# Six FFNs of a two-block model: the exchange of half of x through memory issued by ScalarE instead of SyncE

## The reference, cut to what matters

```python
def swiglu(h, w_gate, w_up, w_down):
    return (jax.nn.silu(h @ w_gate) * (h @ w_up)) @ w_down

def hybrid_layer(x, ...):
    x = x + 0.5 * swiglu(rmsnorm(x, ffn1_norm), ffn1_wg, ffn1_wu, ffn1_wd)
    ...                                   # attention and gated linear attention, x = x + ... @ w_out
    x = x + 0.5 * swiglu(rmsnorm(x, ffn2_norm), ffn2_wg, ffn2_wu, ffn2_wd)
    return x
```

## Time and profile before

| | us |
|---|---|
| median of 3 runs | 1962.08 |
| lowest and highest of them | 1962.0 and 1962.49 |
| the profiled execution | 1962.03 |
| its span in the trace | 1960.2 |

### The profile page before, as it was taken

How to read it: one execution, slowest core, us unless ns; L and a number is a source line. 1 busy time by engine, 2 the same in 40 slices (tenths; PEclk the granted TensorE clock), 3 DMA queues, 4 the chain that set the end, 5 groups by cost and what they waited for, 6 DMA issues and landing times.

```text
span 1960.2 us, 27186 instructions
## 1 busy us (share of the span) xinstructions
PE 1947.4 (99%) x11074; PEld 1638.0 (84%) x11074; DVE 1381.7 (70%) x1714; ACT 1051.5 (54%) x1326; POOL 44.4 (2%) x73
## 2 busy tenths in 40 slices
PE   9999999999999999999999999999999999999998
PEld 8888988888888888888888898788888889878887
DVE  7666987666666697766666679776667666977665
ACT  6545575445544657544644467654454446765444
POOL 0120004000000000000000000000000000000000
PEclk9999999999999999999999999999999999999999
DMA  8765547666666544666566644466666664546662
GB/s 323 259 227 191 171 154 242 226 225 204 241 226 223 187 156 175 233 226 225 180 234 225 220 170 156 151 213 224 228 216 229 225 226 158 174 141 214 225 226 78
DMA packets 162494, 403.06 MB, mean 206 GB/s; under 512 B 94801, under 2 KB 116561, under 8 KB 119873
## 3 DMA queue, kind: packets, MB, share of 16 engines
q1 hardware_dynamic: 160448, 397.19, 58.6%
q0 software_dynamic: 1488, 3.78, 0.6%
q10 hardware_dynamic: 432, 0.35, 0.1%
HBM read 376.12 MB, written 22.81 MB: 204 GB/s over the span
## 4 chain that ended last, share of the span: by engine, by line
PE 92%; DVE 4%; DMA 1%; ACT 1%; SPq 1%; DVEq 1%; issue 0%; ACTq 0%
PE bank L513 87%; DVE w_lo L1479 1%; PE bank L558 1%; DMA raw<-stream 1%; SPq L422 0%; DMA arena<-spill_x 0%; DVE h_lo L1505 0%; PE bank L875 0%; PE bank L755 0%; PE bank L771 0%; DVE arena L1641 0%; PE bank L674 0%; PE bank L894 0%; PE bank L744 0%; PE bank L856 0%
## 5 line engine op out<-in xcount | busy, mean ns | idle before, releaser
L1479 DVE TENSOR_TENSOR w_lo<-raw,w_hi 128x2048 fp32r<-128x2048 f32 x330 | 755.8, 2292 | 356.5 <-ACT w_hi L1036 356.0
L1036 ACT ACTIVATE w_hi<-raw 128x2048 fp32r<-128x2048 f32 x330 | 629.6, 1909 | 267.5 <-PE bank L513 264.3
L513 PE MATMUL bank<-w_hi,h_hi 128*128 128x512 f32 x1552 | 607.7, 392 | 4.0 <-DVE h_lo L1505 2.8
L513 PE MATMUL bank<-w_hi,h_lo 128*128 128x512 f32 x1552 | 604.3, 389 | 0.0
L513 PE MATMUL bank<-w_lo,h_hi 128*128 128x512 f32 x1552 | 604.0, 389 | 0.0
L513 PEld LDWEIGHTS bank<-w_hi,h_hi 128*128 128x128 f32 x1552 | 291.3, 188 | 69.2 <-issue 6.8
L513 PEld LDWEIGHTS bank<-w_hi,h_lo 128*128 128x128 f32 x1552 | 291.3, 188 | 61.3
L513 PEld LDWEIGHTS bank<-w_lo,h_hi 128*128 128x128 f32 x1552 | 291.4, 188 | 59.5
L513 PE MATMUL bank<-w_hi,act_hi 128*128 128x512 f32 x832 | 326.8, 393 | 0.1
L513 PE MATMUL bank<-w_hi,act_lo 128*128 128x512 f32 x832 | 324.1, 390 | 0.0
L513 PE MATMUL bank<-w_lo,act_hi 128*128 128x512 f32 x832 | 323.8, 389 | 0.0
(11 more groups left out here) (245 smaller groups left out, 1359.6 us busy)
## 6 DMA issues: line engine op xcount, KB each, us to landing
raw<-stream SPq DMA_DIRECT2D x331, 1024.0 KB, 4.9
spill<-scratch SPq DMA_DIRECT2D x71, 256.0 KB, 3.6
scratch<-spill SPq DMA_DIRECT2D x71, 256.0 KB, 2.7
spill_x<-x SPq DMA_DIRECT2D x12, 256.0 KB, 2.6
arena<-spill_x SPq DMA_DIRECT2D x12, 256.0 KB, 2.8
arena<-arena SPq DMA_DIRECT2D x32, 64.0 KB, 2.9
arena<-rpb POOLq DMA_DIRECT2D x16, 66.5 KB, 4.4
x<-xt SPq DMA_DIRECT2D x1, 1024.0 KB, 15.2
```

The lines of the kernel that those rows point to most:

```text
L513: last = mm(o, a, r, start=start and n == 0, stop=stop and n == len(pairs) - 1)
L1036: fn(w_hi[u % SLOTS][:, :], raw[u % RAW][:, :], ACT.Copy).then_inc(hi_done, 1)
L1479: tt(w_lo[u % SLOTS][:, :], raw[u % RAW][:, :], w_hi[u % SLOTS][:, :].bitcast(F32), ALU.subtract).then_inc(lo_done, 1)
```

## The change

The four DMAs of each of the six exchanges leave SyncE's loop and go to ScalarE's program. ScalarE issues the two writes between its squares of piece 2 and piece 3, and the two reads between its split of back 0 and its split of front 0 + 3. Waits, sizes, shapes and semaphores are the same. SyncE's loop goes from one load to the next in these places.

```diff
@@ -395,17 +395,6 @@
-            def swap_x(b, L, j):
-
-                no = SWAPPED.index((b, L, j))
-                for t in range(2):
-                    wait_x(sp, x_no(b, L, 2 * j), 2 + t)
-                    sp.dma_start(spill_x[t].rearrange("c p h -> p c h"), x[:, t, 512:D].rearrange("p (c h) -> p c h", c=8)).then_inc(x_out, 16)
-                sp.wait_ge(x_out, 32 * (no + 1))
-                for t in range(2):
-                    sp.dma_start(x_landed[:, t, :].rearrange("p (q n) -> p q n", q=2),
-                                 spill_x[t].rearrange("(q c) (r a) h -> (c r) q (a h)", q=2, a=4)).then_inc(x_back, 16)
@@ -423,13 +412,10 @@
-            swapped = {ffn_use(b, L, j, "front", 0) + RAW: (b, L, j) for b, L, j in SWAPPED}
...
-                if u in swapped:
-                    swap_x(*swapped[u])
@@ -1062,6 +1048,19 @@
+            def swap_out(b, L, j):
+
+                for t in range(2):
+                    wait_x(act, x_no(b, L, 2 * j), 2 + t)
+                    act.dma_start(spill_x[t].rearrange("c p h -> p c h"), x[:, t, 512:D].rearrange("p (c h) -> p c h", c=8)).then_inc(x_out, 16)
+
+            def swap_back(b, L, j):
+
+                act.wait_ge(x_out, 32 * (SWAPPED.index((b, L, j)) + 1))
+                for t in range(2):
+                    act.dma_start(x_landed[:, t, :].rearrange("p (q n) -> p q n", q=2),
+                                  spill_x[t].rearrange("(q c) (r a) h -> (c r) q (a h)", q=2, a=4)).then_inc(x_back, 16)
@@ -1111,8 +1110,11 @@
                     turned_hi(b, L, 2 * j, [0, 1])
-                    squares(v, [2, 3])
+                    squares(v, [2])
+                    swap_out(b, L, j)
+                    squares(v, [3])
                     split(use_of("back", 0))
+                    swap_back(b, L, j)
                     split(use_of("front", 0) + SLOTS)
                     turned_hi(b, L, 2 * j, [2, 3])
```

## The result

| | us |
|---|---|
| before, median of 4 runs (lowest, highest) | 1962.28 (1962.0, 1963.1) |
| after, median of 4 runs (lowest, highest) | 1993.12 (1990.42, 1994.2) |
| ratio, 95% interval | 1.0154 (1.0141 to 1.0166) |
| profiled execution after, and its span | 1992.31, 1990.4 |
| profiled execution before, and its span | 1962.03, 1960.2 |

The kernel became slower by 30.8 us, 1.5%. Forecast were 7.6 us, and a range that ended at 1975. The direction was right, the size was not. The spans differ by 30.2 us, and these are to be found.

A forecast was written before the change was run, and what follows sets the result against it. TensorE's matmuls bound the kernel. Losses of 1.0 us in exchanges 1 and 4, 1.7 in 2, 1.4 in 3, 2.0 each in 5 and 6 make 9.1, less 1.5 lost today: +7.6, 1969.7 us; range 1961.5 to 1975.

The forecast's parts named there:

- What bounds the kernel, and the yardstick: TensorE bounds the kernel; each exchange is judged by its stage, line 558 to line 674, 22.57 us where nothing waits.
- T: Per exchange, start of line 558 (544 after) to VectorE's first block turn of x's right half; no TensorE wait up to 10.7.
- All that can be won is 1.5: All six exchanges: TensorE's waits for x cost about 1.5 us of 1962 today, so no more can be gained.
- each us beyond costs one us of the kernel: In each exchange, every us of T above 10.7 lengthens the kernel by one us.
- Writes, ScalarE, SyncE: Exchanges: writes cost 0 (bounds 0 to 0.4 us), ScalarE's wait 0; SyncE's next load comes earlier, which wins nothing.
- Sharing: Reads beside SyncE's load on two queues: 2.0 us added in exchanges 1, 4, 5, 6; 1.7 in 2 and 3.
- The sentence by the Trainium skill's rule: Engines alternate between queues packet by packet, so the reads would bear the load's whole time, 2.5 to 3 us.
- The fetch: An instruction fetch during the reads of exchanges 5 and 6 comes again and adds 1.0 us to each.
- No change: Rival: the reads, issued first, keep their place ahead of the load; 1960.5 to 1964, best 1962; chance 0.27.
- Faster: Rival: the fetch leaves the reads' way or the reads stand behind nothing, so 1.5 us return: 1960.5; chance 0.05.
- ScalarE issues late: Rival: ScalarE's DMA starts only after its split ends, so reads start 0.6 us later, behind the load: 1973.3; chance 0.13.

The follow-up runs named there:

- f1: Changed kernel, but only the writes go to ScalarE; SyncE issues the two reads and then the next load, as before the change: 1962.86 us, ratio 1.0001.
- g2: Changed kernel, but SyncE's next load also waits until the two writes have landed, so load and reads are issued together: 1987.38 us, ratio 1.0129.
- f3: Changed kernel, but SyncE's next load also waits until the reads have landed: 1962.47 us, ratio 0.9999.
- f4: Changed kernel, but ScalarE issues the load beside the reads, right behind them on the same queue: 1963.08 us, ratio 1.0002.
- g3: Kernel before the change, all on SyncE's one queue, but with the next load issued ahead of the two reads: 1985.26 us, ratio 1.0119.
- g4: Changed kernel plus 40 small matmuls at the start of TensorE's program, which moves later instruction fetches: 1984.05 us, ratio 1.0111.
- h1: Changed kernel, but the second load, the one after next, waits until the reads have landed: 1977.78 us, ratio 1.0081.
- h3: Changed kernel plus 19 small filler matmuls on TensorE before its wait in each of exchanges 2, 3, 5 and 6: 1985.71 us, ratio 1.0116.
- h2: Changed kernel, but the load beside the reads is issued as two DMAs of 512 KB: 1983.94 us, ratio 1.0113.

## Why the prediction was wrong in size

**What bounds the kernel, and the yardstick.** Right. Line 544 to line 660 is longer in all six places, and the six together carry the whole difference. T beyond 10.7 is paid in full: in exchange 1, 12.5 - 10.7 = 1.8, and the stage is 24.4 - 22.6 = 1.8 longer. "All that can be won is 1.5" holds too: no version here is faster than before by a measurable amount. The words "each us beyond costs one us of the kernel" failed where the wait was long: there it cost a slower clock on top.

**Writes, ScalarE, SyncE.** Right. The writes cost 0 (f1). The reads were issued at 308.08 in exchange 1, and the load at 308.44, for which 308.45 was said. In exchange 2 the load came at 492.24, which is the forecast 490.4 plus the 1.8 us that exchange 1 had already lost, 0.69 us ahead of the reads (0.85 was said).

**Sharing: the mis-sized term.** Taken were 2.0 us (1.7 in exchanges 2 and 3). Measured is 12.5 - 9.7 = 2.8 us in exchanges 1 and 4, where nothing else comes in: near the upper bound of 3 that the prediction gave and then dismissed, because it "leaves no worth to any head start". The reasoning for 2.0 was that a read in front keeps a part of its place. The rows show that the first read keeps all of it and the second none, and only the second one counts. The prediction had the fact in hand, that the load becomes free before the second read is issued, and drew nothing from it. By this alone the sum would be 6 x 1.8 = 10.8 less 1.5, so +9.3 us. The sentence by the Trainium skill's rule, 2.5 to 3 us, was nearer than the value taken. Its 32 packets of a read are those of both reads (one read is 256 packets, 16 for an engine), and the packet-by-packet turns that it describes show in g2, but not from 310.5 to 312 of after, where the load is alone.

**The fetch: the step that failed.** It was counted with 1.0 us, in exchanges 5 and 6 alone. In 2 and 3 the prediction did not see it, though it was there, 4.6 and 4.7 us into the stage of before and among the writes; only the T of 10.7 and 10.4 that it started from held its small cost there. Measured, together with the second load: 3.1 in exchanges 2 and 3, 3.6 and 3.2 in exchanges 5 and 6; 13.1 in all. The prediction priced the fetch and a load each by itself, on the traffic of before, and had no term for what two late things do to one engine. It never looked at the second load, 2.6 us behind the first.

**The clock: the missing step.** 7.8 us. No row of before has a wait of TensorE long enough to show it. Nothing in the prediction asked what TensorE does after it has stood still; the cost of it was put at nothing without a reason.

So 10.8 + 13.1 + 7.8 - 1.5 = 30.2 us, against 9.1 - 1.5 = 7.6. Which part is shown: the first by f3, f4 and g3; the second by g4 and h1; the third by h3, in one place. Open is why one engine comes to be late with its reads and then has the second load's packets among them: this is only seen in the packets, and no run tests it. Open is also by what rule the sixteen engines serve two queues: turns of whole DMAs are refuted (h2), the order of issue fits nearly everywhere, and g2 shows packets one for one.

**The rivals.** *No change* is refuted: the first read did keep its place, as it said, and this saved nothing. *Faster* has nothing for it. *ScalarE issues late* is refuted by the timeline of ScalarE: the reads are issued at 308.08 while the split of 306.77, which takes 1.92, still runs:

```profile
306.77 1.92 ACT L1022 ACTIVATE w_hi<-raw 128x2048 fp32r<-128x2048 f32 x1 [0.16 <-issue]
```

The range took its upper end from the one late mechanism that it knew, and had no room for costs that multiply.

## What to carry to other kernels

When a small transfer with somebody waiting for it is taken out of a queue, ask first what large transfer it had been holding back; here that was worth 31 us, and one wait on the load (f3) or one queue for both (f4) gives all of it back. Once TensorE is made to wait for several microseconds, price the matmuls after the wait as well. And a delay of one engine's share is not added to the others but can be multiplied by whatever else is queued by then, so the count of loads issued within the transfer's time belongs into the sum.

## What the runs showed of the hardware

- DMAs on two queues mostly passed in the order in which they were issued: 0.64 MB of a load in 1.5 us with no packet of the other queue between (100.7% of 16 engines), and the second read, issued 0.03 us behind that load, after it. Two half-loads issued ahead of the reads both went first (h2, exchange 2). Where load and first read were issued 0.09 us apart, their packets could alternate one for one, 60 of 8 KB and 61 of 1 KB in 1.2 us (g2).
- Small reads of 256 KB land after 2.8 us by themselves, 5.4 us (median) beside a load that is ahead or between, up to 9.4 us where an instruction fetch and a second load join.
- An instruction fetch of 16 KB among the transfers was worth up to 3.6 us of T per place, where a second load was queued (some 1.5 at most where it was held back), and 40 small matmuls at the start of the kernel decided where it fell.
- After TensorE had stood still for 4.9 to 5.4 us (exchanges 2, 3, 5 and 6 of after) its granted clock went to 1.2 GHz for 3.4 or 6.8 us, at a cost of 1.5 to 2.3 us. After the 1.8 us of exchanges 1 and 4 it did not. In between there is no clean picture: it fell after 2.1 us in h2 (exchange 4) and 2.5 in g3 (exchange 1), and did not after 3.0 in g3 (exchange 6).
- ScalarE's queue issues a DMA while its own activation still runs (308.08 against 308.69).
